# Where the second layer's modulation is computed: moved into the later part of the first layer's mixers

## The reference, cut to what matters

```
mods = (jax.nn.silu(c) @ ada_w + ada_b).reshape(B, 3, 3, 1, D_MODEL)     # ada_w: 1024 x 9216 per layer, f32

def modulate(t, i):
    return t * (1.0 + mods[:, i, 1]) + mods[:, i, 0]

def residual(t, i, out, w):
    return _layer_norm(ALPHA * t + w * (1.0 + mods[:, i, 2]) * out, ln_g[i], ln_b[i])

x = residual(x, 0, _swiglu(modulate(x, 0), ffn_wg[0], ffn_wu[0], ffn_wd[0]), 0.5)
proj = modulate(x, 1) @ w_in
...                                  # o_rw, o_gla, o_ml: three recurrent mixers on proj
mix = jnp.concatenate([o_rw, o_gla, o_ml], axis=-1) @ w_out
x = residual(x, 1, mix, 1.0)
x = residual(x, 2, _swiglu(modulate(x, 2), ffn_wg[1], ffn_wu[1], ffn_wd[1]), 0.5)
```

## Time and profile before

| What | Value |
|---|---|
| Three runs | 1873.8, 1889.33, 1890.78 us; median 1889.33 us |
| Profiled execution: own time, span | 1889.8 us, 1888.0 us |
| TensorE matmuls busy | 1742.9 us, 92% of the span |
| VectorE, ScalarE, GpSimd busy | 977.2, 678.6, 170.6 us (52%, 36%, 9%) |
| Memory to core | 272.36 MB, mean 144 GB/s |
| Chain of work that ended last | 78% TensorE, 11% VectorE, 4% DMA, 4% ScalarE |
| Mean granted TensorE clock | 0.901 of full |

### The profile page before, as it was taken

One profiled execution on the slowest core, in us unless ns is written; L12 is line 12 of the kernel. 1 busy time (PEld: TensorE's weight loads), 2 busy tenths in 40 slices (PEclk: granted clock), 3 DMA queues, 4 the chain that ended last, 5 costly groups with the idle time before them and its releaser, 6 DMA issues.

```text
span 1888.0 us, 33548 instructions
## 1 busy us (share of the span) xinstructions
PE 1742.9 (92%) x14420; PEld 1568.9 (83%) x14420; DVE 977.2 (52%) x1623; ACT 678.6 (36%) x949; POOL 170.6 (9%) x217
## 2 busy tenths in 40 slices
PE   5999998988899788999989999989989996899997
PEld 2899997987768477999979999979867765799997
DVE  2444445585633476555454444458574336655544
ACT  2333334463211435333353333355532123543333
POOL 1000011002001021000110000110020011300011
PEclk9999998999855598999999999999988557899998
DMA  8556545423232145444456555463323112344442
GB/s 325 182 199 212 190 150 188 162 95 118 92 118 68 48 151 189 146 149 153 147 176 211 180 184 174 153 209 108 115 70 129 57 48 79 117 157 146 156 145 73
DMA packets 85203, 272.36 MB, mean 144 GB/s; under 512 B 18976, under 2 KB 21312, under 8 KB 84800
## 3 DMA queue, kind: packets, MB, share of 16 engines
q1 hardware_dynamic: 80640, 267.60, 41.7%
q10 hardware_dynamic: 4416, 2.62, 0.5%
HBM read 263.92 MB, written 6.26 MB: 143 GB/s over the span
## 4 chain that ended last, share of the span: by engine, by line
PE 78%; DVE 11%; DMA 4%; ACT 4%; issue 2%; SPq 0%; POOL 0%; DVEq 0%; ACTq 0%; POOLq 0%
PE psV L1824 11%; PE psV L1826 11%; PE psV L1825 11%; PE psA L1824 9%; PE psA L1825 9%; PE psA L1826 9%; DMA raw<-weights_dram 4%; PE psC L1839 3%; DVE wlo L2098 3%; PE psV L671 2%; ACT whi L1980 1%; PE psY L1839 1%; DVE PJ L1357 1%; PE psV L1849 1%; PE psV L1442 1%
## 5 line engine op out<-in xcount | busy, mean ns | idle before, releaser
L2098 DVE TENSOR_TENSOR wlo<-raw,whi 128x1024 fp32r<-128x1024 f32 x344 | 425.1, 1239 | 459.7 <-ACT whi L1980 457.9
L1980 ACT ACTIVATE whi<-raw 128x1024 fp32r<-128x1024 f32 x344 | 362.2, 1055 | 343.8 <-PE psV L1826 338.7
L1824 PE MATMUL psA<-XH,whi 128*128 128x320 f32 x1200 | 381.6, 318 | 20.3 <-DVE XL L2150 11.5
L1825 PE MATMUL psA<-XL,whi 128*128 128x320 f32 x1200 | 375.9, 313 | 0.0
L1826 PE MATMUL psA<-XH,wlo 128*128 128x320 f32 x1200 | 375.5, 313 | 0.0
L1824 PE MATMUL psV<-XH,whi 128*128 128x320 f32 x848 | 269.9, 318 | 13.2 <-DVE wlo L2098 7.2
L1825 PE MATMUL psV<-XL,whi 128*128 128x320 f32 x848 | 266.0, 314 | 0.0
L1826 PE MATMUL psV<-XH,wlo 128*128 128x320 f32 x848 | 265.7, 313 | 0.0
L1824 PEld LDWEIGHTS psA<-XH,whi 128*128 128x128 f32 x1200 | 230.4, 192 | 35.1 <-issue 27.9
L1825 PEld LDWEIGHTS psA<-XL,whi 128*128 128x128 f32 x1200 | 230.2, 192 | 0.3
L1826 PEld LDWEIGHTS psA<-XH,wlo 128*128 128x128 f32 x1200 | 230.0, 192 | 0.0
(11 more groups left out here) (368 smaller groups left out, 1914.1 us busy)
## 6 DMA issues: line engine op xcount, KB each, us to landing
raw<-weights_dram SPq DMA_DIRECT2D x488, 512.0 KB, 3.3
ZS<-st_rw_dram SPq DMA_DIRECT2D x2, 768.0 KB, 4.7
S<-st_gla_dram ACTq DMA_DIRECT2D x2, 768.0 KB, 5.1
o_glas_dram<-S SPq DMA_DIRECT2D x2, 768.0 KB
o_rws_dram<-ZS SPq DMA_DIRECT2D x2, 768.0 KB
CON<-consts_dram SPq DMA_DIRECT2D x1, 1288.5 KB, 9.5
XT<-xT_dram SPq DMA_DIRECT2D x1, 1280.0 KB, 9.8
yT_dram<-XT SPq DMA_DIRECT2D x8, 160.0 KB
```

The source lines that it names most:

```text
L1824: mm(out, whi[:, n % SPL, k], hi[:, kt], start=first, stop=False)
L1825: mm(out, whi[:, n % SPL, k], lo[:, kt], start=False, stop=False)
L1980: activation(whi[:, n % SPL], raw[:, DENSE[n] % RAW], ACT.Copy).then_inc(hi_done, 1)
L2098: tt(wlo[:, n % SPL], raw[:, DENSE[n] % RAW], whi[:, n % SPL].bitcast(F32), ALU.subtract).then_inc(lo_done, 1)
```

## The change

The spreading of `in_tail` is taken off the first part of `together` and left on the second alone, in both layers. All groups of layer 1's sub-layers 0 and 1 are computed in the second part of layer 0's mixers. So that part has 18 groups (72 chunks) instead of the last 17 chunks of 32; the second part of layer 1's mixers has all 24 chunks of its `in_tail` instead of 12. The up product of layer 1 that had 16 chunks and the three normalizations behind layer 0's output projection, layer 0's second down product and layer 1's first down product have none. The number of chunks, folds and loads stays the same: 144, 36 and 488.

```diff
--- before.py
+++ after.py
@@ -181,8 +181,8 @@
     together = spread([(rw[0], int(k > 1)) for k in range(RW_INVERSE)], first)
     heads, ends = GL_STEPS - GL_FIRST, ML_STEPS - ML_FIRST
     other = (ml + gl) * 6 + su + (ml + gl) * (heads - 6) + su + ml * (ends - heads)
-    together += spread([(rw[0], 1)] * (RW_CHUNKS + RW_SAMPLES - 1), other)
-    out += spread([(step, 1) for step in together], ada_groups(in_tail) if in_tail else [])
+    late = spread([(rw[0], 1)] * (RW_CHUNKS + RW_SAMPLES - 1), other)
+    out += together + spread([(step, 1) for step in late], ada_groups(in_tail))
     out += [("mix", L), ("hi", L)] + rw * 3 + [("lo", L), ("early", L)] + rw
     steps, left = product(("out", L), 1, in_gaps[1])
     out += steps + after(up[1], left)
@@ -195,11 +195,10 @@
         return [(L, i, g) for g in gs]
 
     out = ada_groups(groups(0, 0, 0, 1, 2, 3)) + [("enter", 0)]
-    steps, left = layer_plan(0, groups(0, 0, 4, 5) + groups(0, 1, 0, 1, 2, 3),
-                             (groups(0, 1, 4, 5), groups(1, 0, 2, 3), groups(1, 0, 4, 5)),
-                             groups(0, 2, 0, 1, 2, 3, 4, 5) + groups(1, 0, 0, 1))
+    steps, left = layer_plan(0, groups(0, 0, 4, 5) + groups(0, 1, 0, 1, 2, 3), (groups(0, 1, 4, 5), [], []),
+                             [(L, i, g) for L, i in ((0, 2), (1, 0), (1, 1)) for g in range(6)])
     out += steps
-    steps, left = layer_plan(1, groups(1, 1, 0, 1, 2, 3), (groups(1, 1, 4, 5), [], []), groups(1, 2, 0, 1, 2, 3, 4, 5), left)
+    steps, left = layer_plan(1, [], ([], [], []), groups(1, 2, 0, 1, 2, 3, 4, 5), left)
     return out + steps
```

## The result

The changed kernel took 1914.23, 1916.08, 1918.32 and 1927.19 us, median 1917.2 us; the kernel before, with one more run beside it, has a median of 1881.57 us (1871.8 to 1890.78). The ratio is 1.0184, with a 95% interval of 1.0130 to 1.0238: slower by some 35 us. The forecast was 1930 us, 40 us above the profiled execution of the kernel before, in a range of 1900 to 1957 us. The profiled execution of the changed kernel took 1918.32 us, 28.5 us more than its counterpart. Here and in the experiments the ratios leave out three executions that ran apart from their like (1903.46 and 2372.17 us of the kernel before, 3420.4 us of one experiment), so a ratio is not always that of the two medians.

What follows compares the result with a forecast made beforehand. TensorE was taken to bound the kernel, with matmuls busy for 92% of the span. Terms of -23.4, -9.6, +54.5, +10.1, +5.5, -6, +12.8 and -4 gave +39.9 us on 1889.8 us: 1930 us, range 1900 to 1957 us.

Steps and rivals of the forecast that it cites:

- loads priced at nothing: Layer 0's second part: 72 chunk loads at 199 GB/s don't bind, cost nothing; the ring of four is thin cover.
- a clock priced far too low: Layer 0's second part: two more stretches of 3.4 us at 2.4 GHz, -4 us.
- Where the work can go: Layer 0's second part has no room on TensorE: 54 more chunks cost 54.5 us, 12 more folds 10.1 us.
- Normalizations and up product: These cycles lose 40 chunks: three normalizations gain 3.4 us each, the up product's cycle 16.6 us, together -23.4 us.
- First parts of the mixers: They lose chunks, only those in the chain count: 5.0 us in layer 0, 4.6 us in layer 1, -9.6 us.
- The bank's wait: Layer 0's second part: a group following another at once waits for ScalarE's copy, 11 times 0.5 us, 5.5 us.
- second rival: Waits for the bank are longer, 1951 us; if the ring is also dry, 1966 us; 14%.
- What is hidden: End of layer 0's second part: waits ahead of L1465 and behind `mix` cover some chunks and a fold, about -6 us.
- what the prediction calls right: Layer 0's second part: some 60 us more, 1.01 us per chunk in the chain, clock 0.5 to 0.65.
- first rival: Chunks lift the clock of both second parts to 2.4 GHz: 1840 us, 5%; half of it about 1885 us, 12%.

Runs made afterwards that it cites:

- second profiled execution: The changed kernel run once more, unchanged, beside the kernel before: median 1920.95 us, ratio 1.0186; layer 0's second part took 246.6 us in its profile.
- Groups moved: Against the kernel before, layer 0's mixers compute all of layer 1's sub-layers 0 and 1, spread over the whole list as before: 1896.41 us, ratio 1.0065.
- late spread alone: Against the kernel before, groups in their places, the mixers' modulation spread over the second part alone in both layers: 1913.62 us, ratio 1.0163.
- early spread alone: Against the kernel before, groups in their places, the mixers' chunks spread over the first part alone in both layers: 1880.85 us, ratio 0.9955.
- filled normalization: Against the kernel before, 8 chunks moved from layer 1's mixers into the normalization behind layer 1's output projection: 1897.92 us, ratio 1.0019.
- thin chunks: Against the changed kernel, three of four chunks per group in layer 0's mixers cut to 8 of 256 columns on TensorE: 1912.01 us, ratio 1.0157 to the kernel before.
- thin chunks and small loads: Against the changed kernel, layer 0's mixers with 54 chunks at 8 of 256 columns and 72 loads at 128 of 1024: 1906.52 us, ratio 1.0078 to the kernel before.
- small loads: Against the changed kernel, loads of the 72 chunks in layer 0's mixers bring 128 of 1024 columns: 1928.92 us, ratio 1.0218 to the kernel before.
- groups kept apart: Against the changed kernel, one mixer step put between groups of chunks that followed each other at once: 1925.04 us, ratio 1.0198 to the kernel before.

## Why the prediction was right

*By how much.* Direction and mechanism held. The profiled +28.5 us lie 11.4 us below the forecast of +39.9 us: the cost in layer 0's second part was 8.4 us lower than forecast, the gains in layer 0's first part and in the up product's cycle 4.8 and 2.2 us larger, and against that layer 1's first part gave 5 us less. Within the largest of these terms, loads priced at nothing and a clock priced far too low stood against each other. That the sum came so close is partly luck. The ratio's interval allows 24 to 45 us, and the second profiled execution stood 38 us above the kernel before.

*Where the work can go.* The step that mattered, that layer 0's second part has no room and each chunk there costs its TensorE time, held: +51.7 us for 55 chunks and 13 folds. Groups moved, late spread alone and early spread alone agree, with 1 to 1.4 us per chunk in or out of a second part. Two places don't: the first 17 in layer 0 (188.3 us against 173.8 to 176.0 with one chunk, 0.8 to 0.9 each), and 5 chunks taken out of layer 1's second part in the run with the filled normalization, which gave nothing (188.2 against 188.0 us). That it is TensorE's time and nothing else is argued from the chain; the thin chunks couldn't isolate it, as the clock fell with them.

*Normalizations and up product.* Reading the price off cycles that stood in the trace with and without chunks was the surest step: -3.4 and -16.6 us forecast, -3.3 and -18.8 measured. The 2.2 us are a matter of the clock: layer 1's last cycle, with no chunks in any of the kernels before, changed and moved, took 247.3 us at a mean clock of 0.979 in the first two and 245.5 us at 0.986 in the third, and the up product's cycle ran at 0.987, so the shorter one was its match. For the third, ahead of the projection, -3.4 was an analogy. It seems to have come out smaller: in the kernel with the groups alone moved, layer 1's first part kept its 11 chunks and its stage shrank by 1.7 us.

*First parts of the mixers.* -5 and -4.6 us forecast from the chunks in the chain. Layer 0 gave 9.8 us (2 of them a chunk and a fold between 520 and 522 us, which my sum had in the other part). Layer 1 gave 3.0 us for normalization and first part together, where I had 8. This term was mis-sized. The clock and the gaps explain it as far as it is explained (columns as in the earlier trace rows, before and after):

```profile
1225.00:1437.00 212.00, 191.60 (x2035) 170.05 (x2037) 140.17 (x246) 97.54 (x157) 23.96 (x27) 0.94 0.38 124
```

```profile
1246.00:1455.00 209.00, 181.89 (x1869) 167.83 (x1867) 137.76 (x241) 96.52 (x152) 23.91 (x27) 0.91 0.24 81
```

TensorE has 9.7 us less work and the stage is 3 us shorter. So the chunks had filled gaps, and the clock was higher with them. The prediction counted "only what lies in the chain" as gained and had no term for the clock.

*The bank's wait.* 11 x 0.5 = 5.5 us forecast, 5.7 us measured at 10 places. Nine waits were of 0.5 us and one of 1.1 us; the second rival (2 us each) did not happen, except at the last group's fold (2.73 us). With the waits taken away no gain could be told, so whether the term was a cost of its own is not shown.

*What is hidden.* The wait behind `mix` shrank from 8.38 us to

```profile
699.01 3.57 PE L800 MATMUL psV<-PJ,CON 128*128 128x320 f32 x6 [4.88 <-ACT PJ L882]
```

but this is not all work that found cover: 2.73 us of the difference are the last fold's own wait in the same stretch. The wait of 2.82 us ahead of the mLSTM matmul L1465 (L1464 in the changed kernel) is gone as forecast. Behind this matmul stand two chunks, not three. In all TensorE's idle time at the end fell by 3.6 us (2.82 + 8.38 before, 2.73 + 4.88 after), where 6 were forecast. From this matmul to the one behind `mix` it is 13.06 us before (643.31 to 656.37 in the earlier trace rows) and 12.15 us after, so what stands between them cost nothing.

*Loads.* Priced at nothing, with the ring of four named as thin; TensorE idled 7.2 us for them. With 4 to 5 us of them taken away the stage was no shorter.

*The clock.* This was the term that was furthest off. I took two more stretches of 3.4 us at 2.4 GHz, 4 us; the mean rose from 0.54 to 0.64, the upper end of what the prediction calls right, and by the means of the whole stage 34 to 41 us more ran at 2.4 GHz. What that was worth is not measured. One estimate is the rest of the sum: the forecast of 60 us plus 7 for loads less some 4 for the cheaper pairs, against 51.7 measured, leaves about 11 us beside the 4. Another starts from the kernel with thin chunks and small loads, which had about the clock of the kernel before (0.61 and 0.64 in the stage): 223.3 us and 54 chunks back at 0.93 to 1.01 instead of some 0.25 us are 260 to 264 us, 13 to 24 us more than the two executions took. The price of small matmuls at 1.2 GHz was misread as well. The piece of 6.10 us in the earlier trace rows is not all at 1.2 GHz:

```profile
474.90:481.00 6.10, 6.10 (x124) 6.03 (x128) 2.97 (x6) 0.00 (x0) 0.00 (x0) 0.69 0.02 4
```

From start to start these matmuls take 53 ns ahead of the rise, at 478.7 us, and 30 ns behind it, a ratio of 0.58 and not 0.62. That is a small error beside the choice of 0.7 for the whole. The first rival's mechanism is there in part. The thin chunks show that the full ones are what lifts: with them the clock was 0.50 for 174 us, with full chunks 0.59 to 0.64 there. The Trainium skill, "TensorE: Matmul & The Clock Gate", Part 1, calls the throttled state the default, released by activity. The two runs agree with it in that the clock rose with the fuller chunks, though TensorE was busy in the profile for 153.5 of 174 us with the thin ones, at 1.2 GHz throughout. Against the first rival I had set the first 45 us, chunks alone at 1.2 GHz. That was weak evidence: TensorE was busy for only 23.5 of these 45 us and waited for loads in between. By the two estimates the lift took back between 13 and 24 us. It came with 72 chunks in the stage, not with 32 or 40. In layer 1, with 24 chunks, nothing lifted (0.52 and 0.53).

*Open.* Whether the stage gets shorter when 5 us of waits go, by small loads or by groups kept apart, and if not, why. Both had a lower mean clock in it (0.63, 0.64 against 0.70, 0.68), and the runs of the kernels as a whole (1921.05 to 1930.65 and 1919.14 to 1927.76 us against 1906.67 to 1927.98, on another chip) show no gain, but six runs each can't exclude one of 5 us. That the clock took it back is seen in single profiles only and not shown; what in the order of the work decides it, no run here isolates.

## What to carry to other kernels

Price a move by what the engine does at the new place, not by how the work looks at the old: the chunks of the normalizations had cost 0.4 us each, those of the up product 1.0 us with their folds, and they went to a place where one costs 1 us too, because TensorE was full there and at half its clock. Look in the trace for the same stage with and without the work before estimating it; it is there more often than one thinks. And don't add up waits at the end of such a sum as if each were a gain to be had: here 5 us of waits were real and could be removed, and six runs of each kernel showed no gain.

## What the runs showed of the hardware

- Work that fills gaps can be free. Eleven chunks in layer 1's first part cost nothing that can be measured (211.9 us without, 212.4 us with): TensorE's busy time rose by 4.8 us (187.2 to 192.0), its idle time fell by 4.3 us, and the mean clock was 0.92 without and 0.94 with them. The next 13 cost 14.4 us.
- Chunks alone, with waits for loads between them, took 607 to 634 ns per matmul in the first 28 us, as at a granted 1.2 GHz (631 to 636 between 518 and 565 us) and not as at 2.4 GHz (379 to 403 between 440 and 515 us). The profile's clock column reads 1.00 there, but its records only begin at 45 us: where they are missing, the durations are the better witness.
- Mixed with small matmuls, 72 chunks went with a rise of the clock of a full stage from 0.54 to 0.64; with 54 of them thinned to 8 columns it was 0.50.
- The same kernel was granted 0.70 and 0.68 in one stage in two executions, 6.5 us apart, and the kernel before varied between 1871 and 1901 us in the runs that the ratios rest on. Gains of a few us need many runs to be told from none.
